# State-space stage of a two-block network: features in three fp32r passes, two heads per unit, a group's norm moved into the next group

## What is computed

```python
z, xbc, dt = _split(h @ w_in, ODD_SIZES)                   # 2048, 3072, 64 columns
xs, bm, cm = _split(silu(dwconv1d(xbc, conv_w, conv_b)), (D_INNER, SSD_BC, SSD_BC))
...                                                        # ssd_scan, per direction, chunk and head:
seg = where(tri, cum[t] - cum[s], -inf)
w   = exp(seg) * (C_t . B_s) * dt_s
y   = w @ x + exp(cum) * (C_t @ state)
...                                                        # combine
y = (y + d_skip * x) * silu(z)
y = rmsnorm(y over each of the 4 groups) @ w_out
```

## Time and profile before

| | |
|---|---|
| median of 3 runs | 3250.99 us (3250.58 to 3251.28) |
| profiled execution: time, span | 3250.59 us, 3248.8 us |
| busy over the span | TensorE 2909.9, VectorE 1823.3, ScalarE 1007.2, GpSimd 192.4 us |
| group 0, 1, 2 of the stage | 115.24, 110.23, 112.97 us |
| group 3 and the way to the output projection | 88.92 us |
| first transpose of group 0, start of `ssdout` | at 2506.76 and 2934.12 us |

### The profile page before, as it was taken

One profiled execution on the slowest core, in us unless ns is written; L12 is line 12 of the kernel. 1 busy time (PEld: TensorE's weight loads), 2 busy tenths in 40 slices (PEclk: granted clock), 3 DMA queues, 4 the chain that ended last, 5 costly groups with the idle time before them and its releaser, 6 DMA issues.

```text
span 3248.8 us, 47498 instructions
## 1 busy us (share of the span) xinstructions
PE 2909.9 (90%) x17650; PEld 2344.0 (72%) x17650; DVE 1823.3 (56%) x3194; ACT 1007.2 (31%) x1365; POOL 192.4 (6%) x89
## 2 busy tenths in 40 slices
...
GB/s 261 272 323 247 205 105 121 230 266 213 272 272 237 190 105 143 205 215 215 53 91 60 2 18 92 92 90 92 208 107 78 52 39 52 52 1 104 143 165 81
DMA packets 112963, 468.54 MB, mean 144 GB/s; under 512 B 6984, under 2 KB 64912, under 8 KB 65936
## 3 DMA queue, kind: packets, MB, share of 16 engines
...
...
HBM read 465.05 MB, written 1.06 MB: 143 GB/s over the span
## 4 chain that ended last, share of the span: by engine, by line
issue 50%; PE 36%; DVE 6%; DVEq 4%; ACT 3%; ACTq 1%; PEldq 0%; POOLq 0%; PEld 0%
PE accs L744 9%; PE accs L1084 4%; PE accs L634 4%; PE accs L647 3%; PE accs L648 3%; PE accs L649 3%; DVEq L2440 2%; PE mix L1124 1%; PE mix L1147 1%; DVE normed L86 1%; ACT arena L76 1%; DVE arena L86 1%; PE mix L791 1%; DVE arena L81 1%; PE mix L1114 1%
## 5 line engine op out<-in xcount | busy, mean ns | idle before, releaser
L647 PE MATMUL accs<-normed_r,arena_r 128*128 128x256 f32 (+2 forms) x1864 | 588.3, 316 | 37.7 <-DVEq L1895 22.2
L648 PE MATMUL accs<-arena_r 128*128 128x256 f32 (+1 forms) x2090 | 595.4, 285 | 0.0
L649 PE MATMUL accs<-normed_r,panel_r 128*128 128x256 f32 (+2 forms) x1864 | 583.6, 313 | 0.0
L634 PE MATMUL accs<-normed,panel 128*128 128x256 f32 x2432 | 540.9, 382 | 6.9 <-ACTq L442 3.0
L634 PEld LDWEIGHTS accs<-normed,panel 128*128 128x128 f32 x2432 | 460.6, 191 | 79.5 <-issue 7.0
L647 PEld LDWEIGHTS accs<-normed_r,arena_r 128*128 128x128 f32 (+1 forms) x1864 | 353.3, 190 | 75.4 <-DVEq L1895 22.0
L648 PEld LDWEIGHTS accs<-arena_r 128*128 128x128 f32 x2090 | 396.4, 190 | 2.0 <-issue 0.2
L1319 ACT ACTIVATE arena_r<-panel 128x1024 fp32r<-128x1024 f32 (+1 forms) x240 | 275.3, 1147 | 326.1 <-DMA panel<-w 115.0
L86 DVE TENSOR_TENSOR panel_r<-panel,arena_r 128x1024 fp32r<-128x1024 f32 (+1 forms) x240 | 319.7, 1332 | 96.2 <-ACTq L1320 54.3
L649 PEld LDWEIGHTS accs<-normed_r,panel_r 128*128 128x128 f32 (+1 forms) x1864 | 351.9, 189 | 22.9
L2417 DVE SCALAR_TENSOR_TENSOR arena<-accs,vectors,arena 128x189 f32<-128x189 f32 (+2 forms) x704 | 279.2, 428 | 97.7 <-issue 66.2
...
## 6 DMA issues: line engine op xcount, KB each, us to landing
...
```

What stands on the lines that cost most here:

```text
L634: mm = pe.matmul(acc[b][:, o:o + ntok], w[:, k * PANEL + j * P:k * PANEL + j * P + P], rhs(k), start=(k == 0), stop=(k == KD - 1))
L647: pe.matmul(out, hi[:, k, 0:m], src_hi(k), start=clear and k == 0, stop=False, skip_group_check=True)
L648: pe.matmul(out, hi[:, k, 0:m], src_lo(k), start=False, stop=False, skip_group_check=True)
L649: mm = pe.matmul(out, lo[:, k, 0:m], src_hi(k), start=False, stop=last and k == n - 1, skip_group_check=True)
```

## The change

- **Features** of the stage, dt too, are products in three passes. The input is split in `rms_norm(2)` as in the other layer; its rests lie in freed tables, the ends of panel slots and beside `std`. ScalarE makes the high part of each half-panel (`ssd_high`) into a ring of four buffers, GpSimd the rest, in place. TensorE takes them as 16 items a group (`ssd_item`; 0 to 11 a half-panel's half on 512 tokens, 12 to 15 a half-panel of z): item 0 behind the transposes, 1 and 2 behind C·B, and two in each unit of two heads.
- **Units** take two heads: 8 a group. The broadcast fills 512 columns, ScalarE's and VectorE's operations cover both heads, and the products of the two heads alternate.
- **Convolution** reads PSUM; ScalarE's plain copy goes.
- **The norm.** The mean square of a group is still summed ahead of the next group's transposes, but its root is taken after the next C·B, and `ssd_norm` runs on VectorE behind the next group's masks. Silu of z moves to the start of its own group. `ssdout` waits for `ssd_norm` 2 and 4 instead of the barriers.
- VectorE's runs of independent operations have one drain at their end. `busy` in `rms_norm(2)` goes from 22 to 42 filler matmuls.

```diff
-            order += [Gemm("dt", 1)]
+            order += [Gemm("dt", 1, split=True, kept=True)]
             for g in range(4):
-                order += [Gemm(f"ssdx{g}", 2, 2), Gemm(f"ssdbc{g}", 1, 2), Gemm(f"ssdz{g}", 2)]
+                order += [Gemm(f"ssdx{g}", 2, 2, split=True, kept=True), Gemm(f"ssdbc{g}", 1, 2, split=True, kept=True),
+                          Gemm(f"ssdz{g}", 2, split=True, kept=True)]
...
+        ssd_ring = [X_r[:, :, 0:P], X_r[:, :, P:2 * P], region(0, KD, P, of=arena_r), region(KD * P, KD, P, of=arena_r)]
+        kept_hi["dt"] = cond_slot1_r[:, :, 0:P]
...
+            def ssd_item(g, n):
+                i = n // 2 if n < 12 else n - 6
+                p, u, j = ssd_half(g, i)
...
+                if first:
+                    pe.wait_ge(S("low_made"), split_count(p, 0, u, j))
+                    if p.apa == 2 or j == 0:
+                        pe.wait_ge(free[b], a // BANKS)
+                hi, lo = ssd_hi(g, i), half_panel(p, u, j, slots_r)
+                out = acc[b][:, :] if p.apa == 2 else acc[b][:, j * T:j * T + T]
...
+                for k in ks:
+                    x_hi, x_lo = H_r[:, k, tok], in_lo[2][k][:, tok]
+                    pe.matmul(out, hi[:, k, :], x_hi, start=(k == 0 and (p.apa == 2 or j == 0)), stop=False, skip_group_check=True)
+                    pe.matmul(out, hi[:, k, :], x_lo, start=False, stop=False, skip_group_check=True)
+                    mm = pe.matmul(out, lo[:, k, :], x_hi, start=False, stop=(k == KD - 1), skip_group_check=True)
+                if last:
+                    mm.then_inc(first_used if p.apa == 1 and j == 0 else ready[b], 1)
...
+            def ssd_mean_square(g):
+                pe.wait_ge(S("ssd_gsq"), g + 1)
+                for c in range(4):
+                    mm = pe.matmul(mix[:, 0, 0:T], ones_g[:, :], S_SQ[:, c, :], start=(c == 0), stop=(c == 3))
+                mm.then_inc(S("ssd_gms"), 1)
...
                 xc, (bc_, cc) = S_XC[g % 2], S_BCC[g % 2]
+                if g >= 1:
+                    ssd_mean_square(g - 1)
+                    pe.wait_ge(S("ssd_yz"), g)
                 pe.wait_ge(S("ssd_conv"), g + 1)
                 for s in (1, 2, 3, 0):
...
-                        pe.wait_ge(S("ssd_yz"), g)
...
-                        pe.wait_ge(S("ssd_gstd"), g)
                     for c in range(4):
                         mm = pe.transpose(mix[:, s, c * P:c * P + P], xc[:, c, s * P:s * P + P], ident)
                 mm.then_inc(S("ssd_xT"), 1)
                 if g < 3:
...
+                    ssd_item(g + 1, 0)
...
+                for m in range(8):
+                    pr, d = m // 2, m % 2
+                    n = 8 * g + m
                     if n >= 2:
                         pe.wait_ge(S("ssd_dmin"), n - 1)
...
+                    for hh in range(2):
+                        row = 32 * d + 8 * g + 2 * pr + hh
+                        mm = pe.matmul(mix[:, m % 2, hh * T:hh * T + T], ident[0:64, row:row + 1].to_broadcast([64, P]), dcum[0:64, lat],
+                                       start=True, stop=True)
+                    mm.then_inc(S("ssd_row"), 1)
+                    if m == 1:
+                        pe.wait_ge(S("ssd_state_sb"), g + 1)
+                    if m >= 1:
+                        ssd_out(g, m - 1)
+                    if g < 3:
+                        for item in (2 * m + 3, 2 * m + 4):
+                            if item < 16:
+                                ssd_item(g + 1, item)
+                ssd_out(g, 7)
...
+                part = [slice(64 * hh, 64 * hh + 64) for hh in range(2)]
+                head = [slice(128 * pr + 64 * hh, 128 * pr + 64 * hh + 64) for hh in range(2)]
+                w = [S_DW[n % 2][:, hh, :] for hh in range(2)]
+                for hh in range(2):
+                    pe.matmul(y[part[hh], 0:T], S_ST[:, d, head[hh]], S_CW[n % 2][:, hh, :], start=(d == 0), stop=False, skip_group_check=True)
+                for hh in range(2):
+                    if d == 0:
+                        pe.matmul(y[part[hh], 0:T], S_XT[:, 2, head[hh]], w[hh][:, 0:T], start=False, stop=False, skip_group_check=True)
+                    else:
+                        pe.matmul(y[part[hh], 0:T], S_XT[:, 3, head[hh]], w[hh][:, P:P + T], start=False, stop=False, skip_group_check=True)
+                for hh in range(2):
+                    if d == 0:
+                        mm = pe.matmul(y[part[hh], P:T], S_XT[:, 3, head[hh]], w[hh][:, T:T + P], start=False, stop=False, skip_group_check=True)
+                    else:
+                        mm = pe.matmul(y[part[hh], 0:P], S_XT[:, 2, head[hh]], w[hh][:, 0:P], start=False, stop=True, skip_group_check=True)
...
+            for q in range(4):
+                for i in range(10):
+                    p, u, j = ssd_half(q, i)
+                    pool.wait_ge(S("high_made"), split_count(p, 0, u, j))
+                    pool.tensor_tensor(half_panel(p, u, j, slots_r), half_panel(p, u, j), ssd_hi(q, i), ALU.subtract)
+                    pool.drain().then_inc(S("low_made"), 1)
...
+                act.wait_ge(landed[(p.p0 + u) % SLOTS], 16 * ((p.p0 + u) // SLOTS + 1))
+                if 10 * g + i >= 4:
+                    before, last = (10 * g + i - 4) // 10, (10 * g + i - 4) % 10
+                    q, v, r = ssd_half(before, last)
+                    if q.apa == 1 and r == 0:
+                        act.wait_ge(first_used, G["evengate"].s0 + 4 + 2 * before + v + 1)
+                    else:
+                        wait_ready(act, q, 0, v, r if q.apa == 2 else 0)
+                act.activation(ssd_hi(g, i), half_panel(p, u, j), ACT.Copy).then_inc(S("high_made"), 1)
...
+                ssd_silu_gate(g)
                 act.wait_ge(S("ssd_cb"), g + 1)
                 act.activation(S_BT[:, :, :], mix[:, 0, 0:T].rearrange("p (a b) -> p a b", a=2), ACT.Copy).then_inc(S("ssd_bt"), 1)
+                if g >= 1:
+                    act.activation(S_STD, S_STD, ACT.Sqrt, bias=eps_rms).then_inc(S("ssd_gstd"), 1)
+                act.activation(rms_cols[:, 16:17], one_col, ACT.Exp)
                 act.wait_ge(S("ssd_state"), g + 1)
                 act.activation(S_ST[:, :, :], mix[:, 2:4, :], ACT.Copy).then_inc(S("ssd_state_sb"), 1)
...
+                for m in range(8):
+                    n = 8 * g + m
                     act.wait_ge(S("ssd_row"), n + 1)
                     if n >= 2:
                         act.wait_ge(S("ssd_cw"), n - 1)
...
+                    act.activation(S_ER[n % 2].rearrange("p a b -> p (a b)"), mix[:, m % 2, :], ACT.Exp).then_inc(S("ssd_erow"), 1)
                     act.wait_ge(S("ssd_dmin"), n + 1)
...
+                    act.activation(S_DW[n % 2], S_DW[n % 2], ACT.Exp).then_inc(S("ssd_edec"), 1)
+                    if g < 3:
+                        ssd_features(g + 1, m)
+                        if m < 6:
+                            ssd_high(g + 1, 4 + m)
+                        elif g < 2:
+                            for i in range(2):
+                                ssd_high(g + 2, 2 * (m - 6) + i)
...
+                    act.activation(S_STD, mix[:, 0, 0:T], ACT.Copy).then_inc(S("ssd_conv"), 1)
...
+                outer_taps(dst, acc[b], "ssd_conv_w_2", ssd_channel(g, q), 24, 2).then_inc(free[b], 1)
...
+                if g >= 1:
+                    ssd_norm(g - 1)
...
+                    rows = [32 * d + 8 * g + 2 * pr + hh for hh in range(2)]
+                    for hh, row in enumerate(rows):
+                        for s, (a, b, t0, t1) in enumerate(spans):
+                            dve.eng.tensor_scalar(W[:, hh, a:b], mix[:, m % 2, hh * T + t0:hh * T + t1], dcT[:, s, row:row + 1], 0.0,
+                                                  ALU.subtract, ALU.min)
                     dve.drain().then_inc(S("ssd_dmin"), 1)
...
                     dve.drain().then_inc(S("ssd_cw"), 1)
                     dve.wait_ge(S("ssd_edec"), n + 1)
...
+                    for hh, row in enumerate(rows):
+                        for s, (a, b, t0, t1) in enumerate(spans):
+                            dve.eng.scalar_tensor_tensor(out=W[:, hh, a:b], in0=W[:, hh, a:b], scalar=dtT[:, s, row:row + 1], in1=S_CB[:, d, a:b],
+                                                         op0=ALU.mult, op1=ALU.mult)
                     dve.drain().then_inc(S("ssd_w"), 1)
...
+                    if g < 3 and m < 6:
+                        ssd_conv(g + 1, m)
+                    if m in (3, 5, 7):
```

247 lines of the change are left out of this document (114 added, 133 removed).

## The result

The changed kernel takes 3141.53 us (median of 4 runs, 3139.29 to 3143.29) against 3250.78 before: a ratio of 0.9668 (95% interval 0.9652 to 0.9685), 109 us less where 102 were forecast. The profiled execution has a span of 3137.5 us, 111.3 less than before.

What follows compares the result with a forecast made beforehand. TensorE was taken to bound twelve of sixteen units in groups 0 to 2, a chain through the engines the last four. Terms +5, -81.2 and -25.8 make -102, giving 3149 us; range 3118 to 3192, 8 in 10.

Steps and rivals of the forecast that it cites:

- the likeliest case: The forecast itself for the whole kernel: 3135 to 3165 us, about 58%.
- Features by three passes: Feature matmuls on TensorE: 2.76 us an item, 2.86 for z; sixteen items 44.6 us a group, against 55 before.
- Two heads per unit: Units of groups 0 to 2: broadcast 1.05 us, side-by-side products 1.23, unit 7.8 for what took 10.96; TensorE leads units 0 to 5.
- Its rival: Products of two heads: the two halves of the array do not run side by side; 3186 us, 12%.
- One group: Groups 0 to 2, front through next group's start: 257.2 us together against 338.4, a gain of 81.2.
- The 3 us for half speed: Added in each of groups 0 to 2, because TensorE rests in unit 7 and before the mean square.
- The port: GpSimd's rest parts against VectorE's SBUF access: hidden in units 0 to 5, 2.5 us in unit 7 of groups 0 and 1.
- The full port rival: All 41 rest parts hold VectorE for 2.40 us on the path, 98 us: 3247, no change; 2%.
- the mild one: Milder form of rest parts holding up VectorE: 3165 to 3175 us, 12%.
- Start: Start of the stage, up to the first transposes: 2512 instead of 2506.76, +5 us (bounds +1 and +11).
- Group 3: Last head group with its exit to the output projection: 63.1 us instead of 88.9, a gain of 25.8.
- at half speed two units chain: Units of the last head group: two chain through TensorE, exponential and VectorE in 9.2 us; eight, with entry and last products, 42.3.

Runs made afterwards that it cites:

- the fillers: Changed kernel with filler matmuls where TensorE waits: in unit 7, ahead of the mean square, and in group 3; 3131.64 us.
- The drains: Changed kernel with drains put back behind each of VectorE's four row differences and four weightings of a unit; 3151.91 us.
- the joint kernel: Changed kernel with high parts moved later, one feature item a group moved from front to unit 7, and filler matmuls where TensorE waits; 3108.25 us.

## Why the prediction was right

The measured 3141.53 lies in the range, 7.5 below the predicted 3149, and inside the narrower range of the likeliest case. By its own steps:

- **Features by three passes.** Right, to the size: 2.76 us an item, and TensorE the pace of units 0 to 5. The slopes of a fourth and of a missing pass, 0.92 us in 60 items, show it. VectorE's 6.0 to 6.5 us was some 0.4 too high (5.5 and 6.1 in the kernel with two passes).
- **Two heads per unit.** 1.05 and 1.23 us, as forecast; a unit is 8.0 instead of 7.8, because its two items take 5.73 with their entry (2534.24 to 2539.97), not 5.52. The overlap is shown by taking it away, +23 us. Its rival (12%) falls, and its price was 23 us, not 37, since group 3 gave nothing at the higher clock that it then had. The Trainium skill (TensorEngine Tiling (Array Packing), "Key Properties") says that tiles of the array work on their own, in parallel; 1.23 against 2.31 us agrees.
- **One group.** Front 16.7, 14.9 and 14.8 (14.7; in group 0 it began at half clock), unit 0 6.7 (6.6), unit 6 5.3 (5.1), Square to the next group 5.45 (5.3). The 3 us for half speed were 2.6, 2.7 and 1.8 by the fillers. That the three groups came to 257.5 for 257.2 is partly luck: from the first to the last broadcast each took 52.5 us where 50.7 had been taken (mostly the two items of a unit), and the tails behind it 19.8, 19.4 and 14.4 where 21.6, 21.6 and 17.8 had been, 1.9 to 3.4 us less.
- **The port.** Mis-sized a little, and in the right places: 2.5 a group forecast, 3.4 us of VectorE's time in unit 7, of which 3.0 and 2.7 came back when the rest parts went. Units 0 to 5 hide it. The full port rival falls, the mild one too: a convolution that reads PSUM kept its 1.63 us beside a rest part. The rule cited there from the Trainium skill (SBUF — State Buffer, "SBUF: two separate sides"), whole instructions by turns, agrees: two rest parts of 2.35 us stretched five VectorE operations with two SBUF inputs by 3.4 us.
- **Start.** +3.0 for +5. The input chunks came 1.72 us apart, as forecast, but ScalarE took up `dt` at 2441.90 instead of 2444.4; 1.3 of these 2.5 us are the earlier start of the stage, and 1.2 were too many for `dt`. Its transposes of the rates came at 2462.70, not 2466.5: the chain took 20.8 us where 22.1 had been taken, since the rest parts cost it 2.1 us and not 3.3. From there to the first transposes it was 45.8 for 45.5.
- **Group 3.** Front 13.99 (14); first broadcast to last products 39.3 (2779.92 to 2819.23) where 42.3 were taken. The step that failed in size is "at half speed two units chain": where the clock was at half, two units took 9.4 us, as forecast (9.2), but it was not at half in all of them, 0.71 from the first to the last broadcast. The drains show that VectorE's chain is on this path, and the joint kernel that the clock is too.
- **After the stage.** "All other stages stay as they are" was wrong by 3.4 us, the projection, which now begins at 0.96 instead of 0.50. The exit wait, 4.7 by the prediction, is 4.4 in the profile, and 4.2 in the medians.

Left open is a part of the 109 us. What the runs price is about 40 (three passes, by their slope), 23 (the overlap), 10 (drains), 4 (exit wait) and up to 3 (norm), 80 together. The rest of the change, one set of ScalarE's and VectorE's operations for two heads, one wider broadcast, and the convolution that reads PSUM, was not undone by itself.
